# Prompt attention in a hybrid decoder step: two heads a step, scores as two rounded passes over stacked high and low parts

## The reference, cut to what matters

```python
def stick_breaking(q, k, v, q_pos, k_pos, bias):
    z = (jnp.einsum('bqhd,bkhd->bhqk', q, k).astype(jnp.float32) * (DH_A ** -0.5)
         + bias.astype(jnp.float32)[None, :, None, None])
    mask = k_pos[None, :] < q_pos[:, None]
    log_beta = jax.nn.log_sigmoid(z)
    log_keep = jnp.where(mask, jax.nn.log_sigmoid(-z), 0.0)
    later = lax.cumsum(log_keep, axis=3, reverse=True) - log_keep
    att = jnp.where(mask, jnp.exp(log_beta + later), 0.0)
    return jnp.einsum('bhqk,bkhd->bqhd', att.astype(v.dtype), v)
```

## Time and profile before

| what | value |
|---|---|
| median of 3 runs (lowest, highest) | 3787.16 us (3779.07, 3790.33) |
| span of the profiled execution | 3774.0 us |
| time of that execution outside its span | not listed; the median lies 13.2 us above the span |
| stage of this case in the profile | about 530 to 1272 us |
| PE, DVE, ACT, POOL busy over the span | 92%, 47%, 32%, 8% |

### The profile page before, as it was taken

One profiled execution on the slowest core, in us unless ns is written; L12 is line 12 of the kernel. 1 busy time (PEld: TensorE's weight loads), 2 busy tenths in 40 slices (PEclk: granted clock), 3 DMA queues, 4 the chain that ended last, 5 costly groups with the idle time before them and its releaser, 6 DMA issues. The chain is left out here.

```text
span 3774.0 us, 53101 instructions
## 1 busy us (share of the span) xinstructions
PE 3470.4 (92%) x20032; PEld 3115.9 (83%) x20032; DVE 1756.1 (47%) x3346; ACT 1189.0 (32%) x2192; POOL 303.9 (8%) x796
## 2 busy tenths in 40 slices
PE   7999786999999889999999989988888999999997
PEld 7999674666666679999999978987677999999996
DVE  6444324566656444334334465324644434433436
ACT  5433233455445433111211144112444211111113
POOL 0000113223323000000000000001200000000000
PEclk9999888999999989999999989998988999999998
DMA  4323551222111121111111111223521111111111
GB/s 138 101 101 106 169 166 41 67 49 74 34 35 35 34 82 40 45 39 39 50 40 43 44 29 59 87 71 137 173 60 28 45 44 40 44 44 39 39 50 47
DMA packets 311047, 246.37 MB, mean 65 GB/s; under 512 B 78165, under 2 KB 273049, under 8 KB 310900
## 3 DMA queue, kind: packets, MB, share of 16 engines
q1 hardware_dynamic: 299080, 201.56, 18.2%
q0 software_dynamic: 11824, 42.93, 3.1%
HBM read 185.83 MB, written 58.62 MB: 65 GB/s over the span
## 5 line engine op out<-in xcount | busy, mean ns | idle before, releaser
L449 PE MATMUL ffn_ps<-ffn_in_hi,ffn_w_hi 128*128 128x368 f32 x2112 | 703.4, 333 | 34.6 <-DVE ffn_w_lo L892 22.0
L450 PE MATMUL ffn_ps<-ffn_in_lo,ffn_w_hi 128*128 128x368 f32 x2112 | 701.6, 332 | 0.0
L451 PE MATMUL ffn_ps<-ffn_in_hi,ffn_w_lo 128*128 128x368 f32 x2112 | 700.1, 331 | 0.0
L449 PEld LDWEIGHTS ffn_ps<-ffn_in_hi,ffn_w_hi 128*128 128x128 f32 x2112 | 400.1, 189 | 41.2 <-DVE ffn_w_lo L892 23.1
L450 PEld LDWEIGHTS ffn_ps<-ffn_in_lo,ffn_w_hi 128*128 128x128 f32 x2112 | 399.9, 189 | 0.5
L451 PEld LDWEIGHTS ffn_ps<-ffn_in_hi,ffn_w_lo 128*128 128x128 f32 x2112 | 399.9, 189 | 0.0
L449 PE MATMUL ffn_ps<-ffn_h_hi,ffn_w_hi 128*128 128x368 f32 x1056 | 353.8, 335 | 10.8 <-DVE mix L965 9.9
L451 PE MATMUL ffn_ps<-ffn_h_hi,ffn_w_lo 128*128 128x368 f32 x1056 | 348.9, 330 | 0.0
L450 PE MATMUL ffn_ps<-ffn_h_lo,ffn_w_hi 128*128 128x368 f32 x1056 | 348.1, 330 | 0.0
L965 DVE TENSOR_TENSOR mix<-ffn_ps,mix 128x368 f32<-128x368 f32 x480 | 256.2, 540 | 191.1 <-PE ffn_ps L451 190.4
L836 ACT ACTIVATE ffn_w_hi<-ffn_w_raw 128x1024 fp32r<-128x1024 f32 x132 | 136.1, 1045 | 463.1 <-PE ffn_ps L451 463.1
(11 more groups left out here) (497 smaller groups left out, 6586.3 us busy)
## 6 DMA issues: line engine op xcount, KB each, us to landing
ffn_w_raw<-in_w_ffn_gate_dram SPq DMA_DIRECT2D x44, 512.0 KB, 3.8
ffn_w_raw<-in_w_ffn_up_dram SPq DMA_DIRECT2D x44, 512.0 KB, 3.8
ffn_w_raw<-in_w_ffn_down_dram SPq DMA_DIRECT2D x44, 512.0 KB, 3.7
first_w_raw<-in_w_in_ab_dram SPq DMA_DIRECT2D x27, 512.0 KB, 4.0
rwkv_prep<-xT POOLq DMA_DIRECT2D x4, 2208.0 KB, 7.4
qkv_proj<-qk_out_sb POOLq DMA_DIRECT2D x16, 552.0 KB, 3.0
atts_k_page<-in_cache_k_dram SPq DMA_DIRECT2D x32, 256.0 KB, 3.1
atts_v_page<-in_cache_v_dram SPq DMA_DIRECT2D x32, 256.0 KB, 2.9
```

Of the source, the lines that this page charges most:

```text
L449: pe.matmul(out, w_hi, x_hi, start=first, stop=False)
L450: pe.matmul(out, w_hi, x_lo, start=False, stop=False)
L451: return pe.matmul(out, w_lo, x_hi, start=False, stop=last)
```

## The change

A step now takes both heads of a pair and at most 256 query columns: 25 steps a pair, 100 in all. The tiles `zs`, `keep`, `w` and the PSUM banks hold two heads side by side, so ACT, DVE and the sums still work on up to 512 columns in one instruction; the scaling, whose bias differs by head, becomes two instructions of up to 256 columns.

The scores of a head are two rounded passes. `q_parts` holds the high part of a head's q on partitions 0 to 63 and its low part on 64 to 127. `k_hi` holds the high part of k twice, `k_lo` the low part twice. High q and low q are thus contracted together, once against `k_hi` and once against `k_lo`.

The values of the two heads are two products, each of 64 output columns, written to the two partition halves of the same PSUM columns.

q and k are therefore loaded twice each (8 DMAs for each half of the tokens in place of 3 for a pair), and split: ACT makes the high parts (`q_high`, `k_high`, 3 instructions for each half of the tokens of a pair), POOL the low parts (`q_low`, `k_low`, 2 instructions). For the first pair this stands before the first scores; for later pairs it comes inside the pipeline, and POOL now plays the woven list too. The DMA scratch of the POOL queue is halved.

```diff
-    G = 512
+    G = 256
     steps = []
-    blocks = [(N_META + G, 8), (N_META, 4)]
+    q_blocks = [(N_META + G * b, 2 * b + 2) for b in (3, 2, 1, 0)]
...
-        q_in, k_in, v_in = s.sb("q", [P, 2, TP]), s.sb("k", [P, 2, TP]), s.sb("v", [P, 9, 2, DH])
...
+        q_parts, k_hi, k_lo = (s.sb(n, [P, 2, TP], F32R) for n in ("q_parts", "k_hi", "k_lo"))
+        q_raw, k_raw = q_parts[:, :, :].bitcast(F32), k_lo[:, :, :].bitcast(F32)
...
+            def load_qk(i, part):
+                for to, tile, loaded in ((q_raw, i, q_loaded), (k_raw, i + 4, k_loaded)):
+                    for hh in range(2):
+                        rows = slice(tile * P + 64 * hh, tile * P + 64 * hh + 64)
+                        for half in range(2):
+                            sp.dma_start(to[pair(half), hh, cols_of[part]], qk_in[rows, cols_of[part]]
+                                         ).then_inc(loaded[part], 16)
...
+            def q_low(i, part):
+                cols, upper = cols_of[part], pair(1)
+                pool.wait_ge(hi_made[part], 3 * i + 1)
+                part_waits(pool, parted)
+                pool.tensor_tensor(q_parts[upper, :, cols], q_raw[upper, :, cols], k_hi[upper, :, cols].bitcast(F32),
+                                   ALU.subtract).then_inc(lo_made[part], 1)
+
+            def k_low(i, part):
+                cols = cols_of[part]
+                pool.wait_ge(lo_made[part], 2 * i + 1)
+                part_waits(pool, parted)
+                pool.wait_ge(hi_made[part], 3 * i + 3)
+                part_waits(pool, parted)
+                pool.tensor_tensor(k_lo[:, :, cols], k_raw[:, :, cols], k_hi[:, :, cols].bitcast(F32),
+                                   ALU.subtract).then_inc(lo_made[part], 1)
+
...
-            for _ in rwkv_steps():
-                pass
+            def attention_steps():
+                for t, part in s_steps:
+                    i, n = t // PAIR_STEPS, t % PAIR_STEPS
+                    if part == 0 and n == HIGH_DONE + 2 and i + 1 < NPAIR:
+                        q_low(i + 1, 0)
+                    if part == 0 and n == HIGH_DONE + 3 and i + 1 < NPAIR:
+                        k_low(i + 1, 0)
+                    if part == 0 and n == 1 and 0 < i < NPAIR:
+                        q_low(i, 1)
+                    if part == 0 and n == 2 and 0 < i < NPAIR:
+                        k_low(i, 1)
+                    yield
+
+            weave(plan, rwkv_steps(), attention_steps())
...
-                mm = pe.matmul(att[0:keys, Z, lo:width], k_in[:, hh, k0:k0 + keys],
-                               q_in[:, i % 2, q0 + lo:q0 + width], start=True, stop=not diag, skip_group_check=True)
...
+                for hh in range(2):
+                    q = q_parts[:, hh, q0 + lo:q0 + width]
+                    pe.matmul(att[0:keys, Z, hh, lo:width], k_hi[:, hh, k0:k0 + keys], q, start=True, stop=False,
+                              skip_group_check=True)
+                    mm = pe.matmul(att[0:keys, Z, hh, lo:width], k_lo[:, hh, k0:k0 + keys], q, start=False,
+                                   stop=not diag, skip_group_check=True)
+                    if diag:
+                        mm = pe.matmul(att[0:keys, Z, hh, lo:lo + keys], unit[0:keys, 0:keys],
+                                       not_earlier[0:keys, 0:keys], start=False, stop=True, skip_group_check=True)
...
-                pe.matmul(att[pair(hh), O, lo:width], v_in[0:keys, kt, hh, :],
-                          w[0:keys, n % 2, lo:width], start=first[n], stop=last, skip_group_check=True
-                          ).then_inc(pv_mm, 1)
+                for hh in range(2):
+                    mm = pe.matmul(att[pair(hh), O, 0, lo:width], v_in[0:keys, kt, hh, :],
+                                   w[0:keys, n % 2, hh, lo:width], start=first[n], stop=last, skip_group_check=True)
+                mm.then_inc(pv_mm, 1)
...
+            def q_high(i, part):
+                cols, upper, lower = cols_of[part], pair(1), pair(0)
+                act.wait_ge(q_loaded[part], (i + 1) * 64)
+                part_waits(act, parted)
+                act.activation(k_hi[upper, :, cols], q_raw[upper, :, cols], ACT.Copy).then_inc(hi_made[part], 1)
+                act.activation(q_parts[lower, :, cols], q_raw[lower, :, cols], ACT.Copy).then_inc(hi_made[part], 1)
+
+            def k_high(i, part):
+                cols = cols_of[part]
+                act.wait_ge(k_loaded[part], (i + 1) * 64)
+                part_waits(act, parted)
+                act.wait_ge(lo_made[part], 2 * i + 1)
+                part_waits(act, parted)
+                act.activation(k_hi[:, :, cols], k_raw[:, :, cols], ACT.Copy).then_inc(hi_made[part], 1)
...
-    nc = bacc.Bacc("TRN2", target_bir_lowering=False, num_devices=1)
+    nc = bacc.Bacc("TRN2", target_bir_lowering=False, num_devices=1, dynamic_dma_scratch_size=8192)
```

More of the change, by code:

```diff
@@ L2174, in pair @@
             return slice(64 * hh, 64 * hh + 64)
+        cols_of = (slice(HALF, TP), slice(0, HALF))
         def shape(n):
-            i, hh, q0, width, kt, lo, diag, last = steps[n]
+            i, q0, width, kt, lo, diag, last = steps[n]
             keys = P if kt else N_META
@@ L2301, in _ @@
             pool.memset(al_seq_all[:, :], 0.0).then_inc(state_zero, 1)
+            pool.wait_ge(lo_made[0], 2)
+            pool.wait_ge(state_zero, 2)
+            q_low(0, 1)
+            k_low(0, 1)
             level_masks(pool, levels, levels_made)
@@ L2641, in attention_steps @@
                         scores(t)
-                    if part == 1 and 0 <= t - 3 < NS and not steps[t - 3][7]:
+                    if part == 1 and 0 <= t - 3 < NS and not steps[t - 3][6]:
                         rest(t - 3)
@@ L2719, in attention_steps @@
                 for t, part in s_steps:
+                    i, n = t // PAIR_STEPS, t % PAIR_STEPS
+                    if part == 0 and n == HIGH_DONE + 2 and i + 1 < NPAIR:
+                        q_high(i + 1, 0)
+                    if part == 0 and n == HIGH_DONE + 3 and i + 1 < NPAIR:
+                        k_high(i + 1, 0)
+                    if part == 0 and n == 1 and 0 < i < NPAIR:
+                        q_high(i, 1)
+                    if part == 0 and n == 2 and 0 < i < NPAIR:
+                        k_high(i, 1)
                     if part == 0 and t < NS:
                         keys, lo, width, k0 = shape(t)
-                        head = 2 * steps[t][0] + steps[t][1]
                         act.wait_ge(z_mm, t + 1)
@@ L2748, in attention_steps @@
                                 act.wait_ge(rest_mm, rests[n - 2])
-                        act.activation(keep_hi[0:keys, n % 2, lo:width], keep[0:keys, n % 3, lo:width], ACT.Copy
+                        act.activation(keep_hi[0:keys, n % 2, :, lo:width], keep[0:keys, n % 3, :, lo:width], ACT.Copy
                                        ).then_inc(hi_done, 1)
@@ L2908, in attention_steps @@
                 for t, part in s_steps:
-                    if part == 0 and 0 <= t - 5 < NS and steps[t - 5][7]:
+                    if part == 0 and 0 <= t - 5 < NS and steps[t - 5][6]:
                         n = t - 5
-                        i, hh, q0, width, kt, lo, diag, last = steps[n]
+                        i, q0, width, kt, lo, diag, last = steps[n]
                         dve.wait_ge(pv_mm, n + 1)
-                        dve.tensor_copy(mix[pair(hh), i, q0:q0 + width], att[pair(hh), O, 0:width]).then_inc(out_done, 1)
+                        dve.tensor_copy(mix[:, i, q0:q0 + width], att[:, O, 0, 0:width]).then_inc(out_done, 1)
                     n = t - 2
```

152 lines of the change are left out of this document (82 added, 70 removed).

## The result

The changed kernel is slower by 0.3%: 3795.4 us (median of 20 runs) against 3783.3 (20 runs); the ratio is 1.0027, 95% interval 1.0019 to 1.0036, that is 7 to 14 us more where 33 to 37 less were forecast. The profiled execution of after has a span of 3794.2 us (before 3774.0). Where an execution is listed with both, its time lies about 2 us above its span. So the profiled execution of the kernel before took about 3776 us, some 7 under its median, while that of the change lies at its median: the two traces stand further apart than the kernels do.

The account below looks back on a forecast made before the run. PE was taken as the bound after 595 us: -68 (PE work) + 14 (covers) + 9 (start) + 7 (refills) + 5 (clock) = -33, taken as -37: 3750 us. Forecast's own range 3735 to 3768, range asked for 3718 to 3785.

Parts of the forecast that it names:

- Refills: Six refills of q and k parts: POOL, waiting for ACT, ends inversions late; 7 us cost, bounds 0 and 30.
- PE sets the pace: Stage from 600 to 1250 us: PE, busy 602.6 of 650 us, is the bound; ACT's added work stays hidden.
- Scores and values: PE products: rounded score passes save 29.7 us, values of two heads side by side save 40.9 us.
- covers and clock: Shorter products cover RWKV hops less: 14 us, bounds 0 and 35; PE's mean clock 0.96 for 0.97: 5 us, 0 to 12.
- Start: Stage start: q and k parts delay first scores, SP's state loads and the first blocks; 9 us cost, bounds 3 and 16.
- Scratch: Smaller DMA scratch of the POOL queue: no effect, bounds 0 and 5 us.
- Median over span: Whole kernel: the median lies 13.2 us above the profiled span of 3774.0.
- The rule of the Trainium skill: GpSimd contends with VectorE's two-input instructions: refill subtractions stretch 2 us each, 24 in all; some 6 us more, within bounds.
- A: Rival: value halves pair up and added waits stay small; -60 us, 3727 us; chance 0.18.
- C: Rival: values in two halves run one after the other, 38 us return; 3792 us; chance 0.06.
- B: Rival: PE stops being the bound, hops and inversions set the pace; -12 us, 3775 us; chance 0.16.
- D: Rival: each of six refills holds an inversion by two steps (12 us), and PE with it; 3819 us; chance 0.04.

Follow-up runs that it names:

- e3: The changed kernel without refills: parts made for the first pair of heads only, no loads, copies or subtractions for pairs 1 to 3; ratio 0.9917, 3753.8 us.
- e7: The changed kernel with POOL's low parts for three of the six refills moved behind the inversion in flight (step 21 of a pair); ratio 1.0023, 3787.6 us.
- e16: The kernel before with 18 idle ScalarE copies of 1024 columns into a spare tile, and the small scratch; ratio 1.0006, 3787.9 us.
- e4: The changed kernel with the first rounded pass of each head's scores issued twice, 24 us more PE work; ratio 1.0060, 3805.7 us.
- e9: The kernel before with two heads a step and paired values, full float32 scores, loads and layout of before, no parts; ratio 0.9975, 3777.5 us.
- e1: The changed kernel with full float32 scores again, q and k loaded to both partition halves, no high or low parts; ratio 0.9976, 3773.2 us.
- e11: The changed kernel with the refills' loads only, no copies or subtractions for pairs 1 to 3; ratio 0.9928, 3758.2 us.
- e8: The kernel before with only the scratch for GpSimd's DMA descriptors made smaller; ratio 1.0000, 3782.3 us.
- e18: e9 with RWKV hops weighted 3 in place of 1 in the plan, and sample states stored behind the inversion in flight; ratio 0.9951, 3764.5 us.
- e10: The changed kernel with the refills' ScalarE copies only, no loads or subtractions for pairs 1 to 3; ratio 0.9984, 3777.6 us.
- e17: The changed kernel with all the refills' copies and subtractions for pairs 1 to 3 on GpSimd; ratio 0.9973, 3775.7 us.

## Why the prediction was wrong, step by step

- **Refills: the step that failed.** I put 7 us, they cost 42 (after against e3). I counted only inversions that end late. Of the 42, some 18 go with the subtractions on POOL. These hold the mechanism I named, late inversions (longer in the trace are those of groups 4, 9, 11, 14 and 16; I had named 4, 6, 9 and 14), and one that I had put at nothing, VectorE held up meanwhile. How the 18 divide between the two stays open: e7 repaired three of the inversions and gained nothing clear. The larger part, 22 to 25, is the 18 copies that I had called hidden, because ScalarE is busy half of the time.
- **"PE sets the pace".** It is what made a mean busy share of 55% look like cover. In the kernel before ScalarE's added work is indeed hidden (e16), though no run shows that PE's work counts in full there; in the changed one added PE work counts by half (e4). Each price for ScalarE's and VectorE's added work should have been taken for the new kernel.
- **Scores and values: sizes right, worth wrong.** The products cost as worked out. But 44 us less on PE for values and sums gave 9 (e9, e1), 30 less for scores gave 18 with the loads of the refills in both (e1 to e11) and 22 without (e1 to e3). So what vanished did so with the two-head steps more than with the short score passes. With 68 us less on PE, a start of 6 and a gain of 31 (e3), covers and clock together took 31, where I had 14 + 5. The clock term was too small (0.90 even without refills, where I had 0.96); how much of it is cause and how much follows from the pauses the runs don't say.
- **Without refills** the forecast would have been -40, and e3 is -31, so the rest of the sum was off by 9: 12 too little for covers and clock, 3 too much for the start.
- **Start**: about 6 in place of 9, counted from the stage's first instruction; the chain up to the first scores and to SP's next load is as worked out. The second low parts (541.8 to 548.0) lie in the time until the first blocks come back and cost nothing more. Scratch: nothing, right (e8).
- **Median over span**: the 13 us weren't time outside the span, which is about 2 wherever both are listed. The profiled execution was a fast one, and the median of three runs (3787.2) a high one: that of twenty is 3783.3. This made the time of 3750 look 4 us closer to the result than the change of -37 was.
- **The rule of the Trainium skill.** I weighed it as POOL's subtractions getting longer. They don't: eleven of the twelve take 2.34 to 2.42 us, one 2.87. VectorE pays, by up to 2.1 us an instruction, and `min`, the one held most often, has a single input, where I had thought of instructions with two. The Trainium skill has this too (SBUF — State Buffer, section Who interferes with whom): the pair of ports is locked for a whole instruction and the later one blocks. The trace agrees: `min` starts at 865.87, behind `k_low`'s start, and ends at 867.93, behind its end.
- **Rivals.** A and C fell. B (hops set the pace) put 40 us on covers and clock, the forecast 19; e3 shows 31, between them. D named the right place and sign; it asked for 12 us a refill, there were 7, and its mechanism, the held inversion, is at most the smaller part.

## What to carry to other kernels

An engine's idle share is cover only as long as another engine's queue is full. Before counting added work as hidden, ask what the kernel will look like once the gain is there: if the pacing engine loses a tenth of its work, one microsecond of copying in someone's in-order queue can cost more than its length. When PE work is removed, look where its pauses will be and try to move other work there: e18 did so and kept 19 us, though with a second edit beside it.

## What the hardware showed that I had not expected

- Two pauses of 0.73 and 1.08 us on PE were followed by some 13 us at the lower clock level (e10, 734 to 747), while one of 0.93 us at the same place was not (e3). A stretch with PE's rows at 44.3 of 50 us had a mean granted clock of 0.76 (e9, 880 to 930 us).
- A GpSimd subtraction over two SBUF tiles (2.36 us) holds a one-input VectorE instruction that starts during it (427 ns alone) until its end, so that this takes up to 2.4 us (2.6 in e17); ScalarE's instructions beside it keep their length (the 256-column scaling: 0.457 and 0.465 us within `k_low` of group 9, median 0.466).
- Rounded passes of 256 columns take 0.11 to 0.12 us behind one of their kind, but the first takes 0.17 to 0.22 behind a product of another kind.
